# A two-layer decoder trunk on one core: the mixing of the gating layer moved between its products, with its first weights, first tile and norm row handled earlier

## The chip, the core and the metric

The kernel runs on one core of a Trainium2 chip. Time is the device time of one execution, in microseconds (us). The engines that matter are TensorE (PE, matrix products; its weight loads are shown as PEld), VectorE (DVE), ScalarE (ACT), GpSimd (POOL), and SyncE (SP), which here only starts transfers. Each engine runs its own instructions in the order in which they are written and waits at counters (semaphores) that the others raise.

## The reference

A decoder trunk with two layers on 512 positions of width 1024. Layer 0 mixes with attention and gated linear attention, layer 1 with the spatial gating below (`w_in` is 1024 x 4096, u and v have 2048 columns each). Each layer then has cross-attention into a memory of 256 rows and a mixture of 16 experts of which each position uses two. An RMS norm stands before every part.

```python
def sgu_mixer(h, w_in, ln_g, ln_b, ws, bs, w_out):
    B, S = h.shape[:2]
    z = jax.nn.gelu(h @ w_in)
    u, v = z[..., :SG_WIDTH], z[..., SG_WIDTH:]
    v = layernorm(v, ln_g, ln_b).reshape(B, S // SG_CHUNK, SG_CHUNK, SG_GROUPS, SG_GW)
    w_causal = ws * jnp.tril(jnp.ones((SG_CHUNK, SG_CHUNK), ws.dtype))
    mixed = jnp.einsum('gts,bnsgc->bntgc', w_causal, v) + bs.T[None, None, :, :, None]
    return (u * mixed.reshape(B, S, SG_WIDTH)) @ w_out

for layer in range(DEPTH):
    h = rmsnorm(x, norm_mix[layer])
...
        mix = sgu_mixer(h, sg_w_in[i], sg_ln_g[i], sg_ln_b[i], sg_ws[i], sg_bs[i], sg_w_out[i])
    x = x + mix
...
```

## The kernel before

Positions lie in T = 4 tiles of 128. Every large product is taken in three terms: weights and activations are split into a rounded part (hi) and the rest (lo), and `product` (L222 to L239) issues hi·hi, hi·lo and lo·hi. Weights come in groups of 1024 x 512, in two halves h = 0, 1. SP loads a half into `w_stage` once the lo of the group before it is out (`load`), ACT copies it to `w_hi` once PE has used the half before (`split_hi`, L175; one half alone in `half_hi`, L193), and DVE subtracts it into `w_lo` (`split_lo`, L185; `half_lo`, L199). A product reads 4 tiles x 2 halves, 12 matmuls each. In the text, P0 to P7 are the eight products with `sg_w_in` (P0 to P3 give v, P4 to P7 give u, transposed), and P8 to P11 the four with `sg_w_out`.

The experts of layer 0 (`moe_experts`) end in a loop over extra blocks. After it ACT and DVE each write half of the last result (`finish`), POOL scatters it, and when all is stored SP and ACT load the eight blocks of result rows back (`Combine.load`, L1679).

The gating layer (`sgu_layer`) is one block of code, in which it then does this. ACT and DVE split the weights of P0. DVE adds the result rows to `x_res` (L1692, two adds a tile), ACT squares a tile (L1714) and takes the root (L1720), DVE divides (L1726) and scales by the norm's row (L1728), PE turns the tile (L1740), ACT copies it out (hi, L2184) and DVE subtracts (lo, L2224). On ACT the square and root of tile i + 1 stand ahead of the copy of tile i. P0 works through tiles and halves in a mixed order. Behind each product ACT applies the gelu (L2210, L2213). After P3 the mean and variance of v are taken (ACT squares, L2202), DVE centres v (L2251), POOL multiplies by the layer norm's gain (L2151) and DVE adds its bias (L2256, L2260), with the splits of the coming weights between these. After P7, PE transposes the masked mixing weights `sgu_ws` (L2176) and ACT copies them (L2216).

A second block follows: PE makes the 16 mixing units (L2272, four 128 x 128 matmuls each), DVE adds the mixing bias (L2280) and multiplies by u (L2284), ACT rounds (um_hi, L2290) and POOL subtracts (um_lo, L2296). All engines meet at the end of each block before any starts the next. Then `into_queries` runs P8 to P11, adds them to `x_res`, and goes on to the queries of the cross-attention. `NormTiles` is also used there, and at the start of each mixture of experts (`moe_front`).

## Time and profile before

| | us |
|---|---|
| median of 3 runs (1768.4 to 1770.33) | 1770.12 |
| the profiled execution, its own time | 1771.84 |
| its span, first to last instruction | 1769.8 |
| TensorE busy in the span | 1503.7 (85%) |
| VectorE busy | 991.4 (56%) |
| ScalarE busy | 771.4 (44%) |
| mean granted TensorE clock | 0.914 of full |

The span is the stretch that the trace covers; the execution is 2.0 us longer. The busy shares are averages over very different stages: the gating layer, from the experts' last product at 961 us to the end of P11 at 1309 us, is only a fifth of the span. Times in rows are microseconds from the start of the span.

### The profile page before, as it was taken

To read this page: it belongs to the slowest core of one execution; us is meant where nothing else is said; L and a number is where in the kernel's file an instruction comes from. 1 tells how busy PE (TensorE), PEld (TensorE's weight loads), DVE (VectorE), ACT (ScalarE), POOL (GpSimd) and SP (SyncE) were. 2 spreads that over 40 slices of the span, in tenths; PEclk is the share of its full clock that TensorE was granted. 3 is DMA by queue.
4 is the path that set the end of the run, shared out by engine and by line. 5 is a ranking of instruction groups with operands and counts; after the bars stand their busy time and mean duration, and the time that the engine had idled before them with its cause. 6 is when DMAs were issued, how large, how long until landed. Compare 5 with 4: busy or idle time off the path is not lost. (4 is left out here: it accounts for less than half of the span.)

```text
span 1769.8 us, 19447 instructions
## 1 busy us (share of the span) xinstructions
PE 1503.7 (85%) x7649; PEld 1242.2 (70%) x7649; DVE 991.4 (56%) x1299; ACT 771.4 (44%) x1133; POOL 156.5 (9%) x173
## 2 busy tenths in 40 slices
PE   5789689889899895699996799797989894899994
PEld 4577566667678564699995588676877473899983
DVE  3156447574634526588993522734234526699974
ACT  3222345474423513477773322422133513677761
POOL 1000011200000000111211000504000000121111
PEclk8899799878999997799998799898999897899997
DMA  6523021022342052599994342213212043699985
GB/s 185 83 74 98 2 98 49 1 96 96 113 164 72 1 209 107 179 351 373 366 358 166 118 174 95 71 48 123 90 64 72 0 168 125 227 367 370 369 329 197
DMA packets 105981, 276.52 MB, mean 156 GB/s; under 512 B 36625, under 2 KB 39074, under 8 KB 101026
## 3 DMA queue, kind: packets, MB, share of 16 engines
q1 hardware_dynamic: 69922, 203.68, 32.3%
q10 hardware_dynamic: 26464, 54.79, 8.9%
q0 software_dynamic: 9504, 16.80, 2.5%
q8 instruction: 61, 1.00, 0.2%
q14 instruction: 30, 0.25, 0.0%
HBM read 267.83 MB, written 25.17 MB: 166 GB/s over the span
## 5 line engine op out<-in xcount | busy, mean ns | idle before, releaser
L185 DVE TENSOR_TENSOR w_lo<-w_stage,w_hi 128x2048 fp32r<-128x2048 f32 (+2 forms) x48 | 112.0, 2345 | 307.8 <-ACT w_hi L175 291.6
L175 ACT ACTIVATE w_hi<-w_stage 128x2048 fp32r<-128x2048 f32 (+2 forms) x48 | 86.4, 1812 | 334.7 <-PE bank L239 207.3
L2617 ACT ACTIVATE w_lo<-e_room 128x1536 fp32r<-128x1536 f32 x60 | 89.3, 1488 | 87.1 <-DMA e_room<-in_moe_w_in 85.0
L2621 DVE TENSOR_TENSOR e_wi_lo<-e_room,w_hi 128x1536 fp32r<-128x1536 f32 x60 | 102.9, 1749 | 27.1 <-ACT w_hi L2617 27.1
L2621 DVE TENSOR_TENSOR e_wi_lo<-e_room,w_lo 128x1536 fp32r<-128x1536 f32 x60 | 105.3, 1755 | 20.1 <-ACT w_lo L2617 19.7
L2617 ACT ACTIVATE w_hi<-e_room 128x1536 fp32r<-128x1536 f32 x60 | 86.9, 1500 | 31.9 <-PE bank L239 18.4
L2732 PE MATMUL bank<-e_wi_lo,e_hx_hi 128*128 128x384 f32 x256 | 87.2, 341 | 0.0
L193 ACT ACTIVATE w_hi<-w_stage 128x2048 fp32r<-128x2048 f32 x26 | 49.6, 1913 | 85.6 <-PE bank L239 63.5
L2731 PE MATMUL bank<-e_wi_lo,e_hx_hi 128*128 128x384 f32 x256 | 86.6, 338 | 0.0
L199 DVE TENSOR_TENSOR w_lo<-w_stage,w_hi 128x2048 fp32r<-128x2048 f32 x26 | 59.5, 2288 | 44.1 <-ACT w_hi L193 37.7
L239 PE MATMUL bank<-w_hi,h_mix_hi 128*128 128x512 f32 x128 | 53.3, 416 | 21.4 <-DVE w_lo L185 12.0
L2722 PE MATMUL bank<-ident,e_tok 128*128 128x128 f32 x272 | 40.5, 295 | 25.3 <-PEq L2354 19.8
L236 PE MATMUL bank<-h_sg_hi,w_hi 128*128 128x512 f32 x128 | 51.9, 405 | 10.1 <-DVE w_lo L185 10.1
L239 PE MATMUL bank<-w_hi,um_hi 128*128 128x512 f32 x128 | 51.8, 404 | 9.7 <-PEq L2265 9.7
L2812 ACT ACTIVATE e_hx_hi<-bank 128x512 fp32r<-128x512 f32 x68 | 36.8, 596 | 51.1 <-PE bank L2722 51.0
L2722 PEld LDWEIGHTS bank<-ident,e_tok 128*128 128x128 f32 x272 | 39.1, 207 | 27.9 <-issue 25.8
L2901 DVE TENSOR_TENSOR e_hx_lo<-bank,e_hx_hi 128x512 fp32r<-128x512 f32 x68 | 43.5, 682 | 26.2 <-ACT e_hx_hi L2812 26.2
L2680 POOL DMA_INDIRECT moe_y<-e_tok,moe_slots x28 | 28.1, 1002 | 335.8 <-DVE e_tok L2918 309.7
L2625 POOL DMA_INDIRECT e_tok<-moe_h,moe_slots x32 | 39.5, 1235 | 198.3 <-DVE moe_slots L2574 143.7
L997 PEld LDWEIGHTS bank<-v_sw,probT 128*128 128x128 f32 x304 | 38.1, 194 | 23.3 <-ACT probT L1027 11.6
L239 PE MATMUL bank<-w_hi,x_o_hi 128*128 128x512 f32 x128 | 50.7, 396 | 3.4 <-PEq L1998 3.4
L2731 PE MATMUL bank<-w_hi,e_hx_hi 128*128 128x384 f32 x128 | 48.4, 378 | 5.0 <-DVE e_hx_lo L2901 5.0
(512 smaller groups left out, 4226.4 us busy)
## 6 DMA issues: line engine op xcount, KB each, us to landing
e_room<-in_moe_w_in SPq DMA_DIRECT2D x128, 768.0 KB, 7.7
e_wo<-in_moe_w_out ACTq DMA_DIRECT2D x16, 1536.0 KB, 10.2
e_room<-in_moe_w_out ACTq DMA_DIRECT2D x14, 1536.0 KB, 11.1
w_stage<-in_x_wkv SPq DMA_DIRECT2D x16, 1024.0 KB, 5.1
w_stage<-in_sg_w_in SPq DMA_DIRECT2D x16, 1024.0 KB, 5.4
w_stage<-in_hyb_w_in SPq DMA_DIRECT2D x10, 1024.0 KB, 5.3
w_stage<-in_x_wq SPq DMA_DIRECT2D x8, 1024.0 KB, 5.0
w_stage<-in_x_wo SPq DMA_DIRECT2D x8, 1024.0 KB, 6.0
```

Source lines behind the costliest of these rows:

```text
L175: act.activation(self.w_hi[h][:, :, :cols], self.stage[h][:, :, :cols], ACT.Copy)\
L185: dve.tensor_tensor(self.w_lo[h][:, :, :cols], self.stage[h][:, :, :cols], self.w_hi[h][:, :, :cols], ALU.subtract).then_inc(self.lo_done[ ...
L193: act.activation(self.w_hi[h][:, :, :cols], self.stage[h][:, :, :cols], ACT.Copy).then_inc(self.hi_done[h], 1)
L199: engine.tensor_tensor(self.w_lo[h][:, :, :cols], self.stage[h][:, :, :cols], self.w_hi[h][:, :, :cols], ALU.subtract).then_inc(self.lo_do ...
L236: ins = pe.matmul(banks[b][:w_cols.stop - w_cols.start, :tiles * P], w_part[:, kk, w_cols], x_part[:, k, :tiles * P], start=start, stop=stop)
L239: ins = pe.matmul(banks[b][:, :cols], x_part[:, k, b * P:(b + 1) * P], w_part[:, kk, :cols], start=start, stop=stop)
L2617: act.activation(self.hi[q], self.raw[q][:, :, :], ACT.Copy).then_inc(self.wi_his[q], 1)
L2621: dve.tensor_tensor(self.lo[q][:, :, :], self.raw[q][:, :, :], self.hi[q], ALU.subtract).then_inc(self.wi_los[q], 1)
L2722: ins = pe.transpose(turn_ps[k // 4][:, (k % 4) * P:(k % 4 + 1) * P], hx[:, j, k // KC * KC * P + k % KC:(k // KC + 1) * KC * P:KC], m.ide ...
L2731: pe.matmul(gate_ps[:, 0:DE], x[:, k, :], wt[q][:, kk, 0:DE], start=start, stop=stop)
L2732: ins = pe.matmul(up_ps[:, 0:DE], x[:, k, :], wt[q][:, kk, DE:2 * DE], start=start, stop=stop)
L2901: ins = dve.tensor_tensor(hx_lo[j][:, 4 * g:4 * g + 4, :], turn_ps[g][:, :].rearrange("p (k t) -> p k t", k=4), hx_hi[j][:, 4 * g:4 * g + ...
```

## The change

All of it is in and around the gating layer of layer 1.

1. The 16 mixing units go between the tiles of P5, P6 and P7: units 0 to 3, 4 to 7 and 8 to 15. Their results use the PSUM banks of the product before, units 12 to 15 the banks of units 8 to 11 again. DVE applies bias and gate per unit, ACT and DVE then split, in the same block. The last product's gelu stays in PSUM. POOL has no part in it any more.
2. The layer norm's gain and bias are no longer applied to v. They are loaded as columns (16 numbers in each of 128 partitions), and applied after the mixing, where a column is one channel: mixed · gain + (row sums of the mixing weights · bias + mixing bias). The row sums are two products with ones, in P2, where the transposes of `sgu_ws` now stand too.
3. P8 is begun in the same block, and P9's weights are split in it.
4. P0's weights are split by ACT and DVE at the experts' end, ahead of their `finish`.
5. In P0 each tile is normed, turned, split and multiplied before the next: ACT copies tile i before it squares tile i + 1, DVE takes its lo before the next norm, and PE takes both halves of a tile in a row.
6. The norm's row is loaded before the result rows, into the experts' room. The other small loads wait for the rows, and stand ahead of P1's weights.
7. A first square root on a spare number (`ready_root`) is issued ahead of the norm, here, in `into_queries` and in `moe_front`.
8. P5's weights are taken by DVE behind the statistics, one half between the centrings.

```diff
@@ NormTiles, Residual, Combine
+    def load_gain(self, engine, gain):
+        engine.dma_start(self.gain_row, gain.partition_broadcast(P)).then_inc(self.m.next_gain_in, 16)
+
+    def landed(self, engine):
+        for j in self.ORDER[-2:]:
+            engine.wait_ge(self.m.y_in[j], 16 * (self.layer + 1))
...
+    def ready_root(self, act):
+
+        act.wait_ge(self.eps_set, 1)
+        act.activation(self.spare[:, 0:1], self.eps[:, 0:1], ACT.Sqrt)
...
@@ sgu_layer, sync
-                    nt.load(sp, a["norm_mix"][layer])
+                    combine.landed(sp)
                     sp.dma_start(ws[:, :, :], a["sg_ws"][0].rearrange("g t s -> t g s")).then_inc(ws_in, 16)
+                    with nc.allow_non_contiguous_dma(reason="one gain and one bias per partition"):
+                        sp.dma_start(gcol[:, :], a["sg_ln_g"][0].rearrange("(k p) -> p k", p=P)).then_inc(small_in, 16)
+                        sp.dma_start(bcol[:, :], a["sg_ln_b"][0].rearrange("(k p) -> p k", p=P)).then_inc(small_in, 16)
+                    sp.dma_start(bsr[:, :, :], a["sg_bs"][0].partition_broadcast(P)).then_inc(small_in, 16)
                     m.load(sp, first + NGR)
...
@@ gpsimd
-                    pool.wait_ge(small_in, 48)
-                    for i in range(T):
-                        pool.wait_ge(centred, i + 1)
-                        pool.tensor_tensor(v[:, i, :], v[:, i, :], g[:, :], ALU.mult).then_inc(gained, 1)
+                    pool.memset(ones[:, :], 1.0).then_inc(ws_masked, 1)
@@ tensor
                     turn(0)
-                    turn(1)
                     m.product(pe, first, False, bank(0), hi, lo, ahead=ahead,
-                              order=[(0, 0), (1, 0), (0, 1), (1, 1), (0, 2), (0, 3), (1, 2), (1, 3)])
+                              order=[(h, b) for b in range(T) for h in range(2)])
+                    def mix(k):
+
+                        if k < 12:
+                            pe.wait_ge(read, 4 * NGR + k + 1)
+                        if k == 0:
+                            pe.wait_ge(centred, T)
+                        if k >= 12:
+                            pe.wait_ge(gated, min(k - 3, 12))
+                        for i in range(T):
+                            ins = pe.matmul(bank(NGR + min(k, 11) // 4)[k % 4][:, i * P:(i + 1) * P], v[:, i, k * P:(k + 1) * P],
+                                            wsT[:, k * SGG // KU, :], start=True, stop=True)
+                        ins.then_inc(mixed, 1)
...
+                    between = {2: turn_mix, NGR + 1: mixes({1: [0], 2: [1], 3: [2], 4: [3]}),
+                               NGR + 2: mixes({1: [4], 2: [5], 3: [6], 4: [7]}),
+                               NGR + 3: mixes({1: [8], 2: [9], 3: [10], 4: [11, 12], 5: [13], 6: [14], 7: [15]})}
...
+                    def begin(h, b):
+                        if h == 0:
+                            pe.wait_ge(um_los, KD)
+                            pe.wait_ge(gated, 12 + b + 1)
+
+                    m.product(pe, first + 2 * NGR, False, m.psum[0:4], um_hi, um_lo, last=False, ahead=begin)
@@ scalar
-                    m.split_hi(act, first)
-                    nt.square(act, 0)
-                    nt.take_root(act, 0)
-                    for i in range(1, T):
+                    nt.ready_root(act)
+                    for i in range(T):
                         nt.square(act, i)
                         nt.take_root(act, i)
-                        keep_norm(i - 1)
-                    keep_norm(T - 1)
+                        keep_norm(i)
...
+                        elif n == LAST:
+                            m.half_hi(act, first + n + 1, 1)
+                            part_hi(8, KU)
+                    m.split_hi(act, first + 2 * NGR + 1)
@@ vector
+                    def add_bias(k):
+
+
+                        dve.wait_ge(mixed, k + 1)
...
+                        dve.scalar_tensor_tensor(out=bias[:, k % 2, :], in0=ws[:, gr, :], scalar=bcol[:, k:k + 1], in1=bsr[:, gr, :],
+                                                 op0=ALU.mult, op1=ALU.add).then_inc(bias_made, 1)
...
+                        dve.scalar_tensor_tensor(out=out.rearrange("p (i t) -> p i t", i=T), in0=ps.rearrange("p (i t) -> p i t", i=T),
+                                                 scalar=gcol[:, k:k + 1], in1=bias[:, k % 2, :].unsqueeze(1).to_broadcast([P, T, P]),
+                                                 op0=ALU.mult, op1=ALU.add).then_inc(biased, 1)
...
+                    m.split_lo(dve, first + 2 * NGR + 1)
-        with nc.Block() as block:
-            @block.tensor
-            def _(pe):
-                for k in range(KU):
...
@@ moe_experts, scalar (and the same with split_lo in vector)
                 n = rest(act)
+                if upcoming is not None:
+                    m.split_hi(act, upcoming)
                 act.wait_ge(wo_used, n + L)
```

What stands on three engines where the orders differ. On ACT, from the experts' last result to the first tile of the gating layer (`e_tok` holds the experts' result, `w_stage` the loaded weights, `h_sg_hi` the turned tile), before:

```order
L2834 ACTIVATE e_tok<-bank 128x512
L1679 DMA e_room<-moe_y 128x1024 x4
L2662 UNCONDITIONAL_BRANCH
L2179 UNCONDITIONAL_BRANCH
L175 ACTIVATE w_hi<-w_stage 128x2048 x2
L1714 ACTIVATE sg_v,sg_n_ms<-x_res 128x1024
L1720 ACT_TABLE_LOAD
L1720 ACTIVATE sg_n_root<-sg_n_ms,sg_n_eps 128x1
L1714 ACTIVATE sg_v,sg_n_ms<-x_res 128x1024
L1720 ACTIVATE sg_n_root<-sg_n_ms,sg_n_eps 128x1
L2184 ACTIVATE h_sg_hi<-bank 128x4x128 x2
```

and now:

```order
L175 ACTIVATE w_hi<-w_stage 128x2048 x2
L2996 REGISTER_ALU
L2937 ACTIVATE e_tok<-bank 128x512
L1682 DMA e_room<-moe_y 128x1024 x4
L2761 UNCONDITIONAL_BRANCH
L2245 UNCONDITIONAL_BRANCH
L1726 ACT_TABLE_LOAD
L1726 ACTIVATE sg_n_spare<-sg_n_eps 128x1
L1730 ACTIVATE sg_v,sg_n_ms<-x_res 128x1024
L1734 ACTIVATE sg_n_root<-sg_n_ms,sg_n_eps 128x1
L2250 ACTIVATE h_sg_hi<-bank 128x4x128 x2
```

The two copies of the weights stand ahead of the last result, a table load and a square root ahead of the first square, and the copy of tile 0 ahead of the square of tile 1.

On DVE, from the statistics after P3 (`sg_nmean`, `sg_var`) on, before:

```order
L2243 TENSOR_REDUCE sg_nmean<-sg_vsum 128x4
L2244 TENSOR_SCALAR sg_nmean<-sg_nmean 128x4
L185 TENSOR_TENSOR w_lo<-w_stage,w_hi 128x2048 x2
L2247 TENSOR_SCALAR sg_var<-sg_var 128x4
L2249 RECIPROCAL sg_var<-sg_root 128x4
L2251 TENSOR_SCALAR sg_v<-sg_v,sg_nmean,sg_var 128x2048 x4
L185 TENSOR_TENSOR w_lo<-w_stage,w_hi 128x2048 x2
L2256 TENSOR_TENSOR sg_v<-sg_v,sgu_b 128x2048 x2
L185 TENSOR_TENSOR w_lo<-w_stage,w_hi 128x2048 x2
L2260 TENSOR_TENSOR sg_v<-sg_v,sgu_b 128x2048 x2
L185 TENSOR_TENSOR w_lo<-w_stage,w_hi 128x2048 x2
```

and now (`sg_bias` is the bias of one unit, `bank` its mixing result, `uT` the gelu of u):

```order
L2330 TENSOR_REDUCE sg_nmean<-sg_vsum 128x4
L2331 TENSOR_SCALAR sg_nmean<-sg_nmean 128x4
L2333 TENSOR_SCALAR sg_var<-sg_var 128x4
L2335 RECIPROCAL sg_var<-sg_root 128x4
L2338 TENSOR_SCALAR sg_v<-sg_v,sg_nmean,sg_var 128x2048
L199 TENSOR_TENSOR w_lo<-w_stage,w_hi 128x2048
L2338 TENSOR_SCALAR sg_v<-sg_v,sg_nmean,sg_var 128x2048 x3
L199 TENSOR_TENSOR w_lo<-w_stage,w_hi 128x2048
L2350 SCALAR_TENSOR_TENSOR sg_bias<-sgu_ws,sgu_b,sg_bs_row 128x128
L2355 SCALAR_TENSOR_TENSOR bank<-bank,sgu_g,sg_bias 128x512
L2363 TENSOR_TENSOR uT<-uT,bank 128x512
L2350 SCALAR_TENSOR_TENSOR sg_bias<-sgu_ws,sgu_b,sg_bs_row 128x128
```

P5's weights moved behind the statistics, the bias adds over 2048 columns are gone, and the first units come before P6's weights.

On PE, where the gating block ended before (`sg_wsT` holds the transposed mixing weights):

```order
L236 MATMUL bank<-h_sg_lo,w_hi 128x512
L2176 MATMUL bank<-ident,sgu_ws 128x128 x8
L2129 UNCONDITIONAL_BRANCH
L2266 UNCONDITIONAL_BRANCH
L2272 MATMUL bank<-sg_wsT,sg_v 128x128 x64
L2265 UNCONDITIONAL_BRANCH
L1789 UNCONDITIONAL_BRANCH
L239 MATMUL bank<-w_hi,um_hi 128x512
L239 MATMUL bank<-w_lo,um_hi 128x512
L239 MATMUL bank<-w_hi,um_lo 128x512
```

and where it ends now, at the last row of P8 and the first of P9:

```order
L239 MATMUL bank<-w_hi,um_lo 128x512
L2155 UNCONDITIONAL_BRANCH
L1803 UNCONDITIONAL_BRANCH
L239 MATMUL bank<-w_hi,h_sg_hi 128x512
L239 MATMUL bank<-w_lo,h_sg_hi 128x512
L239 MATMUL bank<-w_hi,h_sg_lo 128x512
```

The transposes and the 64 mixing matmuls no longer stand between two ends of blocks; one end of a block is left, between P8 and P9, instead of two ahead of P8.

## Rows read from the trace of the kernel before

**Rows 1.** ScalarE, timeline: start, us, instruction, times, idle before it.

```profile
955.17 0.50 ACT L2819 ACTIVATE e_actT<-bank 128x384 f32<-128x384 f32 x1
...
969.27 3.71 ACT L175 ACTIVATE w_hi<-w_stage 128x2048 fp32r<-128x2048 f32 x2 [7.24 <-PEq L2662]
...
979.57 1.28 ACT L1720 ACT_TABLE_LOAD   x1
980.87 0.29 ACT L1720 ACTIVATE sg_n_root<-sg_n_ms,sg_n_eps 128x1 f32<-128x1 f32 x1
...
986.40 1.06 ACT L2184 ACTIVATE h_sg_hi<-bank 128x512 fp32r<-128x512 f32 x2
```

**Rows 2.** VectorE, timeline.

```profile
961.44 0.69 DVE L2918 COPY e_tok<-bank 128x512 f32<-128x512 f32 x1 [4.83 <-PE bank L2743]
971.22 4.49 DVE L185 TENSOR_TENSOR w_lo<-w_stage,w_hi 128x2048 fp32r<-128x2048 f32 x2 [9.09 <-ACT w_hi L175]
975.62 3.88 DVE L1692 SCALAR_TENSOR_TENSOR x_res<-e_room,moe_wgt,x_res 128x1024 f32<-128x1024 f32 x3
...
989.12 1.28 DVE L2224 TENSOR_TENSOR h_sg_lo<-bank,h_sg_hi 128x512 fp32r<-128x512 f32 x2
...
1131.92 13.13 DVE L185 TENSOR_TENSOR w_lo<-w_stage,w_hi 128x2048 fp32r<-128x2048 f32 x2
```

**Rows 3.** The first result rows' transfers, issued at 966.2 us: time to landing.

```profile
DMA to landing us min/median/max: 4.5/4.6/4.8
```

**Rows 4.** The last result rows' transfers, issued at 967.5 us: time to landing.

```profile
DMA to landing us min/median/max: 8.9/10.1/11.3
```

**Rows 5.** Table loads of the norms' roots: ns min/median/max, first and last start.

```profile
L1720 ACT ACT_TABLE_LOAD  x4: 1283/1283/1283, 673.6 to 1464.1; - x4
```

**Rows 6.** TensorE, timeline, at its waits and one product's start.

```profile
983.00 1.97 PE L1740 MATMUL bank<-ident,sg_v 128*128 128x128 f32 x8 [21.61 <-DVE sg_v L1728]
...
990.55 0.77 PE L239 MATMUL bank<-w_hi,h_sg_hi 128*128 128x512 f32 x1 [0.51 <-DVE h_sg_lo L2224]
...
1138.64 0.77 PE L236 MATMUL bank<-h_sg_hi,w_hi 128*128 128x512 f32 x1 [10.07 <-DVE w_lo L185]
...
1191.50 16.16 PE L2272 MATMUL bank<-sg_wsT,sg_v 128*128 128x128 f32 x128 [4.35 <-PEq L2129]
...
1217.34 0.77 PE L239 MATMUL bank<-w_hi,um_hi 128*128 128x512 f32 x1 [9.68 <-PEq L2265]
```

**Rows 7.** Windows: us, busy of PE, PEld, DVE, ACT, POOL, clock, DMA share, GB/s.

```profile
1016.60:1106.20 89.60, 89.60 (x385) 72.09 (x384) 18.68 (x10) 25.96 (x41) 0.00 (x0) 1.00 0.40 135
...
1138.60:1144.00 5.40, 5.36 (x13) 4.23 (x14) 5.40 (x1) 0.00 (x0) 4.30 (x1) 0.50 0.58 194
...
1217.30:1222.40 5.10, 5.06 (x12) 4.03 (x13) 0.00 (x0) 0.00 (x0) 0.10 (x1) 0.50 0.79 182
```

**Rows 8.** Windows of the mixing units alone (L2272): PE, PEld, clock, DMA.

```profile
1193.50:1194.50 1.00, 1.00 (x7) 1.00 (x7) 0.50 0.00 0
...
1202.00:1204.00 2.00, 2.00 (x20) 2.00 (x19) 1.00 0.00 0
```

**Rows 9.** The centring's instructions: ns min/median/max.

```profile
L2251 DVE TENSOR_SCALAR sg_v<-sg_v,sg_nmean,sg_var x4: 1341/3468/5656, 1118.3 to 1126.4; 128x2048 f32<-128x2048 f32 x4
```

**Rows 10.** Groups by line, 960 to 1320 us: busy us, mean ns; idle before.

```profile
L2280 DVE TENSOR_TENSOR bank<-bank,sg_bs_row 128x512 f32<-128x512 f32 x16 | 11.1, 693 | 2.7 <-PE bank L2272 2.7
...
L2213 ACT ACTIVATE uT<-bank 128x512 f32<-128x512 f32 x16 | 8.2, 597 | 0.0
```

**Rows 11.** DMA issues of the whole run: count, KB each, us to landing.

```profile
w_stage<-in_sg_w_in SPq DMA_DIRECT2D x16, 1024.0 KB, 5.4
...
mem_gains<-in_norm_mem ACTq DMA_DIRECT2D x2, 4.0 KB, 6.7
k_gains<-in_x_knorm ACTq DMA_DIRECT2D x2, 1.0 KB, 6.5
...
mix_gain<-in_norm_mix SPq DMA_DIRECT2D x1, 4.0 KB, 10.6
```

More of the change, by code:

```diff
@@ L1757, in into_queries @@
         out = xn
-        res = Residual(m, f"{nm}_mix", first, parts, x_in)
+        res = Residual(m, f"{nm}_mix", first, parts, x_in, begun=back is not None)
         nt = NormTiles(m, f"{nm}_n", t, res, xn, gb)
@@ new lines, in turn_mix @@
+                    def turn_mix(h, b):
+                        if (h, b) == (0, 2):
+                            pe.wait_ge(read, 8)
+                            pe.wait_ge(ws_masked, 2)
+                            for q in range(2):
+                                for j in range(4):
+                                    ins = pe.transpose(bank(1)[q][:, j * P:(j + 1) * P], ws[:, 4 * q + j, :], m.ident[:, :])
+                                ins.then_inc(turned, 1)
+                        if (h, b) == (1, 1):
+                            pe.wait_ge(ws_out, 2)
+                            for q in range(2):
+                                ins = pe.matmul(bank(1)[2 + q][:, :], ones[:, :], wsT[:, 4 * q:4 * q + 4, :].rearrange("p g t -> p (g t)"),
+                                                start=True, stop=True)
+                            ins.then_inc(summed, 1)
@@ new lines, in gate, with part_lo @@
+                    def gate(k):
+                        dve.wait_ge(biased, k + 1)
+                        dve.wait_ge(read, 4 * NGR + k + 1)
+                        other = bank(NGR + k // 4)[k % 4][:, :]
+                        dve.tensor_tensor(uT[:, k, :], uT[:, k, :], other, ALU.mult).then_inc(gated, 1)
+                    def part_lo(k0, k1):
+                        for k in range(k0, k1):
+                            dve.wait_ge(um_his, k + 1)
+                            dve.tensor_tensor(half(k)[1], uT[:, k, :], half(k)[0], ALU.subtract).then_inc(um_los, 1)
@@ L2253, in _ @@
+                    centre(0)
+                    m.half_lo(dve, first + NGR + 1, 0)
+                    for i in range(1, T):
+                        centre(i)
+                    m.half_lo(dve, first + NGR + 1, 1)
+                    for k in range(4):
+                        add_bias(k)
+                        gate(k)
                     m.split_lo(dve, first + NGR + 2)
-                    for i in range(2):
-                        dve.wait_ge(gained, i + 1)
-                        dve.tensor_tensor(v[:, i, :], v[:, i, :], b[:, :], ALU.add)
+                    for k in range(4, 8):
+                        add_bias(k)
+                        gate(k)
@@ L2257, in _ @@
+                    part_lo(0, 4)
                     m.split_lo(dve, first + NGR + 3)
-                    for i in range(2, T):
-                        dve.wait_ge(gained, i + 1)
-                        dve.tensor_tensor(v[:, i, :], v[:, i, :], b[:, :], ALU.add)
-                    m.split_lo(dve, first + 2 * NGR)
-        um_hi, um_lo = m.split_pair(um_ctx, "um", k=KU, side="right")
-        m.phase()
-        mixed, biased, gated, split, lo_out = (m.psem(f"sg_{s}") for s in ("mixed", "biased", "gated", "split", "lo_out"))
@@ new lines, in _ @@
+                    for k in range(8, 12):
+                        add_bias(k)
+                        gate(k)
+                    part_lo(4, 8)
+                    m.half_lo(dve, first + 2 * NGR, 0)
+                    for k in range(12, KU):
+                        add_bias(k)
+                    for k in range(12, KU):
+                        gate(k)
+                    m.half_lo(dve, first + 2 * NGR, 1)
+                    part_lo(8, KU)
+                    m.split_lo(dve, first + 2 * NGR + 1)
```

172 lines of the change are left out of this document (94 added, 78 removed).

## The prediction, made before the change was run

> **What bounds the kernel now.** I read first where TensorE waits in the stretch from the experts' last product (it ends at 961.4 us) to P8, with the timelines of ScalarE and VectorE beside it, then the windows for the clock. Inside P1 to P4 nothing waits: four products take 89.6 us, 22.4 each, at the full 2.4 GHz [rows 7]. What can be won lies at four places, which rows 6 show by their waits: 21.61 us ahead of the first tile, some 6 more to P0 at 990.55; 10.07 us ahead of P6; and 4.35 and 9.68 us on either side of the mixing. After the 10 us waits the clock is at its low level, 1.2 GHz, for 5.4 and 5.1 us [rows 7]; even the 4.35 us wait is followed by low clock within the mixing [rows 8].
>
> The first place is a chain. The result rows are issued at 966.2 and the first two land 4.6 us later, at 970.8 [rows 3], but VectorE adds them at 975.62, straight behind 4.49 us of weight split that itself waited for ScalarE's 3.71 us [rows 1, 2]. Then come a square, a table load of 1.28 us and the root [rows 1, 5]. PE turns tile 0 from 983.00 to 984.97 [rows 6], ScalarE copies it only at 986.40 [rows 1], behind the square of tile 1, VectorE takes the lo only at 989.12 [rows 2], behind tile 1's norm and an add. The third place: four centrings of 3.5 us mean, of which the shortest, begun before GpSimd's multiplies, took 1.34 [rows 9], and then 13.13 us for two splits [rows 2] that take 4.49 elsewhere. So two engines that work at the same time on large float32 tiles slow one another here, and P6 waits for it. The fourth is a serial section of two ends of blocks.
>
> **The change part by part.** Savings are counted as how much earlier a product starts.
>
> Start of P0. After the loop ScalarE is free at 955.67 [rows 1]. Its 3.71 us of copies, VectorE's last half of 2.25 behind them, and up to 1 us to leave the loop end at 961.6 to 962.6. The last result's `finish` waits behind them on both engines, and it could start at 961.44 [rows 2]; POOL's scatter and both row queues wait for it in turn. That is a delay of 0.2 to 1.2 us, and I take 1.3, since the scatter's own start may not align. The first add then comes at 970.8 + 1.3 + 0.3 = 972.4 instead of 975.6: 3.2. The table load, issued while the rows are under way, gives 1.3. From the end of tile 0's transposes to P0 there were 990.55 - 984.97 = 5.6 us; in the new order two copies (1.06 together, rows 1), the second half of a lo (0.68, half of the 1.28 in rows 2) and handovers make about 2.1: 3.5. Sum: 8.0, so P0 starts near 982.6. The norm's row leaves the chain, but the root came later than it did.
>
> P0 itself. Its start at the low clock stays. One more transposition lies inside it (half of 1.97 at full clock, rows 6): -1.0. The rest of a tile's chain (square, root, scale, copy, lo) is about 5 us against 5.6 us of products per tile, so I take no wait, and up to 2 as the bad end. The order by tiles releases half 0 of the weights only 2.8 us before P0's end instead of 5.6, and copy and split take 1.9 + 2.3 + 0.15: P1 waits 1.55 longer. Left: 5.4.
>
> P2: eight transposes moved in (1.0) and two products with ones, each of 512 columns as a whole mixing unit, 0.8: -2.6. Left: 2.8. VectorE's two copies of the sums and the waits on the small loads are hidden by P2's second half, 8 us.
>
> P4 to P7. A mixing unit is eight records, ten records take 1 us at the full clock [rows 8]: 0.8 us, 16 units, 12.8 in all. Unit 0 also waits for P4's first gelu: the copy of P5's second half 1.9, a table load 1.3 and a gelu 0.6 [rows 10] after P4's end, against 2.8 us of products, so 1.2. After P5: 2.8 - 3.2 - 1.2 = -1.6. The centrings at 1.34 are over before P4 ends, and one half split between them is ready for P5. P6's weights then come behind unit 3, with 7 us to spare: the 10.07 us wait goes, and with it half of 5.4 at the low clock, 2.7. Left: 11.2 at P6's start, and after the twelve units in P6 and P7 (9.6) 1.6. So P7 ends near 1184.5, against 1186.1.
>
> VectorE's load there: per unit a small bias, then two passes of 0.69 [rows 10], 1.7 us; PE gives one per 3.6. It is hidden while P5 to P7 run. GpSimd's 16 subtractions move to VectorE, where 8 fit into P6 and P7 and 8 into P8.
>
> The serial section. From 1186.1 to P8's start at 1217.34 are 31.2 us, and half of 5.1 at the low clock is 2.6 [rows 6, 7]. Now P8 waits only for the gelu (0.6) and the gate (0.7) of unit 12, with handovers 1.5. Left: 1.6 + 31.2 + 2.6 - 1.5 = 33.9.
>
> **A wait that the change adds.** P9's second half of weights can be copied only when P8 has used its own, so copy 1.9, split 2.3 and the end of the block (0.5) and SP's last issue (0.4) follow P8's end with PE idle, though half 0 is ready: -5.1. All queues wait there. After 4.35 us there were about 3 us of low clock [rows 8], after 10.07 there were 5.4 [rows 7]; between the two I take 3.4, half of it lost: -1.7. Left: 27.1.
>
> The other roots. Two `moe_front` and the `into_queries` of layer 1 have a table load in the chain of tile 0 (four in rows 5, one of them the gating layer's own), with PE idle soon behind. 3 x 1.28 = 3.8, less 0.2 where the last tile's add waits for PE: 3.6.
>
> Small loads. P1's weights were needed at 1011 and now at 1006.6, when P0's half 0 is free. SP starts them behind the last rows, 967.5 + 11.3 + 1.3 = 980.1 [rows 4], behind four small loads. A column load has 2048 separate numbers. Loads of 1024 and of 256 separate numbers landed after 6.7 and 6.5 us [rows 11], so nearly all of it is latency that overlaps. At 6.7 each and strictly one after another, weights would land at 980.1 + 4 x 6.7 + 5.4 = 1012.3, 5.7 late. Overlapped they are in time; I take 0, and 5.7 as the end of the range.
>
> **Sum**: 27.1 + 3.6 = 30.7. The profiled execution took 1771.84, so 1741.1; the median lies 1.7 lower, so 1739.4.
>
> **Rivals.** *The columns are late.* One after another, as above, or one of them at the 10.6 us of a load queued behind 4 MB [rows 11]: +5.7, 1745.1. Against it, SP's transfers overlapped in every stage. *The columns cost by the number* (this one ends slower). If the 6.5 us of the 256 numbers were their price, 2048 cost 52 us, and two 104; P1's weights land at 1090, 83 us after they are needed, and the kernel takes 1739.4 + 83 = 1822. It decides from about 26 us a load. Against it stands the load of 1024 numbers in 6.7. The Trainium skill, "DMA: Bandwidth & Descriptors", Rules for kernel authors, speaks against such a load: a last dimension that isn't contiguous becomes one descriptor per element, and one is told to rearrange. By that rule there are 2048 descriptors a load here; the rows show no price for one beyond latency. *The norms' 3.6 us are taken back* by a transfer that the experts wait for: 1743. *The units wait.* PE takes its work in order, and each unit stands behind a gelu of the product before or a gate; at 0.5 us for each of 16 the kernel takes 8 more, 1747.4. Against it, VectorE needs 1.7 us of 3.6. *A table switch costs more than its record.* If each switch cost its record twice, four of them would give 5.1 more: 1734.3. Against it, the root starts at 980.87, 0.02 us behind the table's end [rows 1]. The Trainium skill ("ScalarE: Activation LUTs", What ACT_TABLE_LOAD costs) gives about 2.66 us for every switch, 1.28 and a drain; by that the four are worth 10.6 rather than 5.1.
>
> **How the numbers follow.** Forecast 0.58 (own range 1736 to 1743), norms taken back 0.14, columns late 0.10, units wait 0.08, table 0.04, columns by the number or a like jam 0.03, and 0.03 for a change whose parts give each other nothing. A measurement of this kernel can tell some 0.2%, 3.5 us, from no change. Faster by more: 0.95; within: 0.02; slower: 0.03. The range takes the table's 1734.3 at the low end, and 1745 with part of the norms or of the units' waits at the high end: 1733.5 to 1748. It leaves out the last two cases and the worst sums.
>
> **What would show it.** P0 should start 8 us earlier relative to the experts' last product, P1 show one wait of 1.5 us, P5 to P7 last 26.8, 25.6 and 28.8 us at full clock with no wait for weights, P8 start 1.5 us after P7, and one wait of 5 us stand between P8 and P9 with low clock behind it. VectorE's centrings should take 1.3 us each. No table load should stand between a square and a root. A wait of PE for weights ahead of P1 longer than 3 us would show the columns late; waits spread over P5 to P7 would show the units; P8 at a low clock would mean that I priced the handover too low. If P6 still waits for its weights, then it was not GpSimd that slowed VectorE.

## The result, and the profile of the changed kernel

| | before | changed |
|---|---|---|
| median of 4 runs, us | 1769.26 (1766.39 to 1770.33) | 1739.65 (1735.79 to 1745.9) |
| the profiled execution, its own time | 1771.84 | 1736.91 |
| its span | 1769.8 | 1735.1 |
| TensorE busy in the span | 1503.7 (85%) | 1493.7 (86%) |
| VectorE busy | 991.4 | 983.2 |
| mean granted TensorE clock | 0.914 | 0.927 |

The ratio is 0.9844, with a 95% interval of 0.9821 to 0.9866: 27.6 us less than 1769.26 by the ratio, 23.7 to 31.7 by its interval, and 29.6 between the medians. Forecast were 1739.4 and 30.7 us.

The timeline of TensorE in the changed kernel, at its waits. Columns: start in us, duration in us, instruction, result from inputs, times, and in brackets the idle time ahead of it with what ended it. These rows answer to [rows 6].

```profile
951.37 5.39 PE L2846 MATMUL bank<-e_wo,e_actT 128*128 128x512 f32 x12 [1.01 <-ACT e_actT L2922]
973.05 1.97 PE L1754 MATMUL bank<-ident,sg_v 128*128 128x128 f32 x8 [16.29 <-DVE sg_v L1742]
977.12 0.77 PE L239 MATMUL bank<-w_hi,h_sg_hi 128*128 128x512 f32 x1 [2.10 <-DVE h_sg_lo L2306]
1005.85 0.50 PE L239 MATMUL bank<-w_hi,h_sg_hi 128*128 128x512 f32 x1 [1.60 <-DVE w_lo L185]
1102.26 1.16 PE L2200 MATMUL bank<-sg_wsT,sg_v 128*128 128x128 f32 x8 [1.17 <-ACT uT L2290]
1182.65 0.47 PE L239 MATMUL bank<-w_hi,um_hi 128*128 128x512 f32 x1 [1.55 <-DVE uT L2363]
1210.50 0.77 PE L239 MATMUL bank<-w_hi,h_sg_hi 128*128 128x512 f32 x1 [5.22 <-PEq L2155]
1284.66 1.60 PE L1754 MATMUL bank<-ident,x_xn 128*128 128x128 f32 x8 [3.68 <-DVE x_h_lo L1908]
```

Read from the top: the experts' last product, tile 0's turn, P0, P1, mixing unit 0 (inside P5), P8, P9, and a tile's turn behind P11. The waits of 21.61, 10.07, 4.35 and 9.68 us of [rows 6] have become 16.29, nothing, nothing and 1.55, and there is one new wait of 5.22.

The products between them are told by windows of the changed kernel: P5, P6 and P7. Columns: stretch, its length, busy time of PE, PEld, DVE, ACT and POOL with instructions, granted clock, DMA share, GB/s.

```profile
1098.40:1125.80 27.40, 26.23 (x130) 21.55 (x129) 11.84 (x15) 7.19 (x8) 0.00 (x0) 1.00 0.28 90
1125.80:1151.70 25.90, 25.90 (x130) 21.50 (x129) 14.00 (x18) 7.82 (x10) 0.00 (x0) 1.00 0.26 82
1151.70:1181.10 29.40, 29.40 (x160) 24.74 (x158) 18.14 (x26) 7.85 (x10) 0.00 (x0) 1.00 0.21 73
```

The clock is at 2.4 GHz throughout (1.00), and P6 and P7 have no idle time. VectorE is busy for 12 to 18 us of each. Its centrings answer to [rows 9] (min/median/max in ns), and the first one and one half of P5's split stand where the order puts them:

```profile
L2338 DVE TENSOR_SCALAR sg_v<-sg_v,sg_nmean,sg_var x4: 1341/1342/1347, 1090.9 to 1097.2; 128x2048 f32<-128x2048 f32 x4
1090.90 1.35 DVE L2338 TENSOR_SCALAR sg_v<-sg_v,sg_nmean,sg_var 128x2048 f32<-128x2048 f32 x1
1092.49 2.29 DVE L199 TENSOR_TENSOR w_lo<-w_stage,w_hi 128x2048 fp32r<-128x2048 f32 x1 [0.24 <-ACT w_hi L175]
```

**One clock for all kernels.** Between two executions the times from the start of the span drift, so I count from the start of the experts' last product (956.01 and 951.37 here, the rows with L2743 and L2846). The earlier 4.64 us are then set apart. "Turn" is the last row of the first fence.

| us behind the experts' last product | P0 | P8 | P9 | turn |
|---|---|---|---|---|
| before | 34.5 | 261.3 | 286.5 | 360.5 |
| changed | 25.8 | 231.3 | 259.1 | 333.3 |
| less | 8.8 | 30.1 | 27.4 | 27.2 |

Of the 27.2 us, 1.3 are the table load of the norm behind P11, so the gating layer gave 25.9. The norms outside it gave 1.3 each: TensorE's rows of the two kernels are 36.8 us apart ahead of layer 1's `moe_front` and 38.2 behind its norm, and 0.8 and 2.1 in layer 0. That is 25.9 + 3.9 = 29.8 us, and the medians differ by 29.6; the ratio gives 27.6, so the agreement to 0.2 us is partly chance. The two profiled executions are 34.9 apart, and the rest is not the change's. 2.5 us arose inside layer 0's experts, whose code is the same: TensorE's stretch from their first turn to their last product took 238.1 us in the profiled execution of before, 235.6 in that of the changed kernel, and 235.4 to 238.3 in the twelve kernels below. Another 5.0 us arose in layer 1's cross-attention, between the turn (31.8 us apart) and the 36.8, where the same 16 transposes took 3.39 us before and 1.97 now, and 3.4 us went back behind the last norm.

### The profile page after: what moved, and what is told of

The parts are those of the page before. It is cut to its first block and busy times, and to the rows that moved or that the text cites. A ratio compares the mean times of both kernels' runs of the same rounds, so it can differ in the third digit from the quotient of the medians.

```text
span 1735.1 us, 19494 instructions
## 1 busy us (share of the span) xinstructions
PE 1493.7 (86%) x7653; PEld 1233.3 (71%) x7653; DVE 983.2 (57%) x1329; ACT 770.5 (44%) x1138; POOL 114.0 (7%) x154
## 2 busy tenths in 40 slices
DMA packets 109822, 274.44 MB, mean 158 GB/s; under 512 B 40722, under 2 KB 43171, under 8 KB 105123
## 5 line engine op out<-in xcount | busy, mean ns | idle before, releaser
L185 DVE TENSOR_TENSOR w_lo<-w_stage,w_hi 128x2048 fp32r<-128x2048 f32 (+2 forms) x42 | 89.7, 2148 | 244.2 <-ACT w_hi L175 227.1
L175 ACT ACTIVATE w_hi<-w_stage 128x2048 fp32r<-128x2048 f32 (+2 forms) x46 | 82.5, 1807 | 297.6 <-PE bank L239 201.2
L199 DVE TENSOR_TENSOR w_lo<-w_stage,w_hi 128x2048 fp32r<-128x2048 f32 x32 | 73.3, 2289 | 64.4 <-ACT w_hi L193 37.2
L193 ACT ACTIVATE w_hi<-w_stage 128x2048 fp32r<-128x2048 f32 x28 | 53.5, 1913 | 93.1 <-PE bank L239 62.2
L239 PE MATMUL bank<-w_hi,h_sg_hi 128*128 128x512 f32 x192 | 78.3, 408 | 8.9 <-PEq L2155 5.2
L239 PE MATMUL bank<-w_lo,h_sg_hi 128*128 128x512 f32 x192 | 77.0, 401 | 0.0
L239 PE MATMUL bank<-w_hi,h_sg_lo 128*128 128x512 f32 x192 | 77.0, 401 | 0.0
L2825 PEld LDWEIGHTS bank<-ident,e_tok 128*128 128x128 f32 x272 | 38.7, 207 | 27.9 <-issue 25.8
```

Source lines behind the costliest of these rows:

```text
L175: act.activation(self.w_hi[h][:, :, :cols], self.stage[h][:, :, :cols], ACT.Copy)\
L185: dve.tensor_tensor(self.w_lo[h][:, :, :cols], self.stage[h][:, :, :cols], self.w_hi[h][:, :, :cols], ALU.subtract).then_inc(self.lo_done[ ...
L193: act.activation(self.w_hi[h][:, :, :cols], self.stage[h][:, :, :cols], ACT.Copy).then_inc(self.hi_done[h], 1)
L199: engine.tensor_tensor(self.w_lo[h][:, :, :cols], self.stage[h][:, :, :cols], self.w_hi[h][:, :, :cols], ALU.subtract).then_inc(self.lo_do ...
L239: ins = pe.matmul(banks[b][:, :cols], x_part[:, k, b * P:(b + 1) * P], w_part[:, kk, :cols], start=start, stop=stop)
L2825: ins = pe.transpose(turn_ps[k // 4][:, (k % 4) * P:(k % 4 + 1) * P], hx[:, j, k // KC * KC * P + k % KC:(k // KC + 1) * KC * P:KC], m.ide ...
```

## The experiments

**The changed kernel once more**

> The changed kernel once more, as the other end for the kernels that are run beside it. The sum of the prediction gives a ratio of 0.983 to the kernel before (30.7 us less); if part of the 34.9 us between the two profiled executions was chance (3.3 us stand ahead of the gating layer in the trace, of which the table load ahead of the first mixture of experts explains 1.3), the ratio stays at 0.983 and does not go to 0.980.

1739.91 us, ratio 0.9841 (0.9816 to 0.9866). P0, P8, P9 and the turn stand at 25.9, 231.4, 259.2 and 333.4 us on the common clock: here the stage repeats to 0.1 us, although the times of whole executions spread over 12 us. It does not always. In two kernels further down the same order of work stands ahead of P8, and P8 starts at 232.0 and 232.4 us, because the low clock at P0's start lasted 5.6 and 6.2 us instead of 4.1. The turn moves by another 1.5 us with the low clock in P9. So effects of two microseconds and more are read below from that clock, those under 1.2 us are not shown by one pair of traces, and the ratio is used only where effects are large.

**The mixing in a row, in the same block**

```diff
-                    between = {2: turn_mix, NGR + 1: mixes({1: [0], ...
+                    between = {2: turn_mix}
...
+                    for k in range(KU):
+                        mix(k)
```

The units use the banks of P6 in turn; VectorE takes all splits first, then biases and gates, then the differences.

> The changed kernel, but all 16 mixing units stand in a row behind P7, still in the same block and still with the columns and VectorE's differences: only the interleaving is undone. Theory: P5 to P7 fall from 27.4, 25.9 and 29.4 us to 22.4 us each (15.5 us back), and behind P7 VectorE does 16 units of 0.35 + 0.75 + 0.65 us and 8 differences of 0.6 us before P8 can begin, 33 us in place of a wait of 1.6 us, with a low clock behind it (1 to 3 us): 17 to 20 us more than the changed kernel, ratio to the kernel before about 0.994. Rival: the 27 us that the gating layer lost came from the dropped block ends and GpSimd's part, not from the interleaving: less than 8 us more than the changed kernel, ratio under 0.989.

1766.71 us, ratio 0.9998 (0.9985 to 1.0011): nearly the whole gain is gone, 24.4 us of it by the common clock at P9 and 25.6 at the turn (P0, P8, P9, turn: 25.7, 253.5, 283.6, 358.9). The rival is dead: it gave the interleaving less than 8 us. All other parts of the change are in this kernel, and they leave it at the time of before. P0 still starts 8.8 us earlier than before and P6 waits for nothing, but P8 starts only 7.8 us earlier, and behind P9's wait, which stays, 1.6 are left at the turn. My size, 17 to 20 us, was short by some 6. VectorE's timeline behind P7, which ended at 1162.7:

```profile
1166.61 2.29 DVE L199 TENSOR_TENSOR w_lo<-w_stage,w_hi 128x2048 fp32r<-128x2048 f32 x1 [10.79 <-ACT w_hi L193]
1168.82 0.35 DVE L2343 SCALAR_TENSOR_TENSOR sg_bias<-sgu_ws,sgu_b,sg_bs_row 128x128 f32<-128x128 f32 x1
1197.26 4.89 DVE L2361 TENSOR_TENSOR um_lo<-uT,um_hi 128x512 fp32r<-128x512 f32 x8
```

The first unit's bias comes 6.1 us behind P7, because half 1 of P8's weights, which ScalarE copies only after the gelu, stood ahead of it in VectorE's order. Then come 28.4 us for 16 units, 1.78 each, and 4.9 of differences. P8 started at 1202.25, 39.6 us behind P7 and not 33. I had written the queue and not walked it.

**GpSimd's multiplication left out of the kernel before**

```diff
-                        pool.wait_ge(centred, i + 1)
-                        pool.tensor_tensor(v[:, i, :], v[:, i, :], g[:, :], ALU.mult).then_inc(gained, 1)
```

> The kernel before without the multiplication of v by the layer norm's gain, which GpSimd did beside VectorE's centrings: this work is left out and nothing takes its place. Theory: the centrings took 1.34 to 5.66 us each because GpSimd worked beside them; without it each takes 1.34 us, VectorE reaches the split of P6's weights some 8 us earlier, and the 10.07 us wait at P6 falls to 0 to 2 us: 8 to 10 us less. Rival: the wait at P6 comes from the order of VectorE's work (statistics, split of P5, centrings, bias in a row); then it stays over 5 us.

1755.54 us, ratio 0.9931 (0.9908 to 0.9954), some 12 us less, where I had expected 8 to 10 and left out the low clock behind the wait. VectorE, and below it, from the kernel before, the same instructions and GpSimd's:

```profile
1116.07 5.12 DVE L2247 TENSOR_SCALAR sg_v<-sg_v,sg_nmean,sg_var 128x2048 f32<-128x2048 f32 x4
1121.10 2.29 DVE L185 TENSOR_TENSOR w_lo<-w_stage,w_hi 128x2048 fp32r<-128x2048 f32 x1
```

```profile
1118.31 13.68 DVE L2251 TENSOR_SCALAR sg_v<-sg_v,sg_nmean,sg_var 128x2048 f32<-128x2048 f32 x4
1131.92 13.13 DVE L185 TENSOR_TENSOR w_lo<-w_stage,w_hi 128x2048 fp32r<-128x2048 f32 x2
1119.82 23.08 POOL L2151 TENSOR_TENSOR sg_v<-sg_v,sgu_g 128x2048 f32<-128x2048 f32 x4 [135.91 <-DVE sg_v L2251]
```

Four centrings take 5.12 us in place of 13.68, and TensorE waits for nothing from P1 to the mixing. From the second tile's turn to the mixing it took 190.8 us (985.55 to 1176.34) in place of 203.4: 12.6, which is the 10.07 of the wait and the 2.7 of the low clock behind it. The order of VectorE's work was the same, so the rival is dead. The Trainium skill, "SBUF — State Buffer", SBUF: two separate sides, has GpSimd share one pair of ports with VectorE as an exclusive lock: where VectorE runs in a two-port mode, or reads two inputs from SBUF beside a GpSimd operation that reads SBUF, one engine stands still for a whole instruction of the other. The trace agrees in kind: the longest centring took 4.3 us more than the shortest, and all of it went with GpSimd's work; the lock itself no run here shows.

**The spare root alone, in the kernel before**

```diff
+                nt.ready_root(act)
                 for i in range(3):
                     nt.square(act, i)
```

> The kernel before with the spare square root alone, ahead of all norms (gating layer, queries twice, mixtures of experts twice). Theory: each table load of 1.28 us that stands between the first square and its root goes into idle time of ScalarE, and each is on the path: five times 1.3, or 6.4 us less, the queries of layer 0 counted only if they wait for the root; the prediction took 4.9 us (1.3 in the gating layer, 3.6 for three of the others), ratio 0.9972. Rival: a load costs more than its own 1.28 us because the engine drains around it, 2.7 us each: 10 to 13 us less, ratio 0.994. Other rival: the loads only move (the next gelu or exponential must load its table anyway), ratio 1.000.

1762.7 us, ratio 0.9972 (0.9958 to 0.9986), 4.9 us less: the predicted sum of 1.3 and 3.6. The price of a drain (10 us and more) lies outside the interval, and so does a mere move of the loads. In the gating layer only 0.8 us arrived at the first turn (978.94 - 952.72 = 26.2 against 27.0) and 1.2 at P0. VectorE's row says why:

```profile
977.40 0.16 DVE L1728 RECIPROCAL sg_n_rstd<-sg_n_root 128x1 f32<-128x1 f32 x1 [1.18 <-DMA sg_junk<-in_norm_mix]
```

With the table load gone the norm's row is the last to come. The Trainium skill, "ScalarE: Activation LUTs", What ACT_TABLE_LOAD costs, gives 2.66 us a switch, 1.28 of them the load; what a hidden load brought here was 1.3 us at each of three norms, the load alone.

**The norm's row asked for in the gating block again**

```diff
-                    combine.load_gain(sp, m.a["norm_mix"][layer + 1])
...
+                    combine.load_gain(sp, a["norm_mix"][layer])
                     combine.landed(sp)
```

> The changed kernel, but the norm's row is asked for at the start of the gating block again, behind SyncE's four result rows. Theory: in the kernel before with the spare root alone, the first norm then waited 1.2 us for this row, although VectorE's adds ended late there (976.2); in the changed kernel the adds end 11 us earlier against the request, so the row (7 to 8 us from its request, some 1.7 us behind the rows' own) is the last to come: the first norm waits 1.5 to 3 us and P0 starts that much later than 25.8 us behind the experts' last product; the time is 1.5 to 3 us over the changed kernel. Rival: the row lands beside the result rows and costs nothing.

P0 at 31.0 us in place of 25.8, P8 at 236.3 in place of 231.3: 5.2 and 5.0 us more, over the 3 that I gave it at most. The timing (0.9855, 0.983 to 0.988) does not contradict that and does not show it. The row took 11.2 us from its request at 966.33, behind eight result rows of the same size, not 7 to 8:

```profile
977.53 0.16 DVE L1740 RECIPROCAL sg_n_rstd<-sg_n_root 128x1 f32<-128x1 f32 x1 [5.81 <-DMA e_room<-in_norm_mix]
```

**P0's weights split in the gating block again**

```diff
-                    m.split_hi(act, upcoming)
...
+                    m.split_hi(act, first)
                     nt.ready_root(act)
...
+                    m.split_lo(dve, first)
                     combine.add(dve, 0, 0)
```

> The changed kernel with P0's weights split in the gating block again, ahead of the norm. Theory: VectorE adds the first row only after 4.5 us of splits, P0 starts 3.4 us later than the 25.8 us behind the experts' last product, less the 1.0 us by which the rows are asked for sooner since the result's last half isn't queued behind the split: 3.2 us more. Rival: the rows' landing, 4 us behind their request, hides most of the split: under 1 us more.

P0 at 29.8 us, P8 at 235.2: 4.0 and 3.9 us more than the changed kernel; 1744.17 us, ratio 0.9865 (0.9844 to 0.9887). The theory holds with a term that was 0.8 us too small; the rival does not.

**P0's old order**

```diff
-                              order=[(h, b) for b in range(T) for h in range(2)])
+                              order=[(0, 0), (1, 0), (0, 1), (1, 1), (0, 2), (0, 3), (1, 2), (1, 3)])
```

with the turns, copies and norms in the order of before.

> The changed kernel with P0's order as it was before (two tiles turned ahead, root of the next tile ahead of the copy, mixed halves). Theory: P0 starts 3.5 us later against the experts' last product (29.2 us behind its start in place of 25.8), but P0 has no turn more inside it and P1 no wait of 1.6 us, which gives 2.6 us back: the time is that of the changed kernel within 1.5 us (the net of the term was 1.0 us). Rival: the order is worth its full 3.5 us.

P0 at 28.5 us, 2.75 later; but P8 at 230.8, 0.5 us earlier. Ratio 0.9844 (0.9822 to 0.9865), that of the changed kernel. Part 5 of the change gives nothing that can be seen: the earlier start is paid back inside P0 and at P1. Which of the two orders is ahead is not shown, because the low clock at P0's start was not equally long. Windows from 3 to 6 us behind P0's start, of this kernel and of the changed one:

```profile
983.19:986.19 3.00, 3.00 (x14) 2.36 (x14) 2.63 (x5) 1.45 (x3) 0.00 (x0) 0.98 0.99 338
980.12:983.12 3.00, 3.00 (x16) 2.48 (x16) 2.13 (x2) 0.18 (x1) 1.20 (x2) 0.81 1.02 180
```

A granted clock of 0.81 in place of 0.98 over 3 us is the whole 0.5 us.

**Eight more columns**

```diff
+                        for j in range(8):
+                            sp.dma_start(more[:, j, :], a["sg_ln_g"][0].rearrange("(k p) -> p k", p=P)).then_inc(more_in, 16)
```

> The changed kernel with eight more loads of the gain's column behind the two that it has, ahead of P1's weights in SyncE's queue; nothing reads them. The second column held SyncE for 2.7 us. Theory: a column load costs its queue 2.5 to 3 us, eight push the request for P1's weights from 5.0 us behind the first small load to some 26 us, past the 16 us of slack that P1's weights have, and P1 waits 4 to 8 us for them. Rival: the column loads run beside the rest at well under 1 us each (the first took 0.58 us): P1 waits 1.6 us as before. Other rival: a column costs by its 2048 numbers, over 8 us each: P1 waits over 40 us.

SyncE's own timeline:

```profile
974.79 2.76 SPq L2163 DMA_DIRECT2D sgu_b<-in_sg_ln_b  x1
977.59 11.35 SPq L2165 DMA_DIRECT2D sg_wsT<-in_sg_ln_g  x8
989.00 1.36 SPq L2166 DMA_DIRECT2D sg_bs_row<-in_sg_bs  x1
990.41 67.17 SPq L163 DMA_DIRECT2D w_stage<-in_sg_w_in  x8
```

Eight loads held the queue for 11.35 us, 1.4 each, where I had expected 2.5 to 3: the 2.7 us of the second column were not the price of a column. By the common clock P1's weights were asked for 11.7 us later than in the changed kernel, the first half landed some 5.5 us on, near 996, and P1 still waited 1.60 us, for the split. The one execution of this kernel took 1733.48 us. The theory fails, and so does the price by the number; the first rival had the wait right and its price, well under 1 us, too low. A column is cheap enough that ten are hidden. The Trainium skill, "DMA: Bandwidth & Descriptors", Rules for kernel authors, warns of one descriptor for each number. The trace agrees on the count: this kernel moved 57233 packets under 512 B and the changed one 40722, which is 2064 for each of the eight loads of 2048 numbers. The price in this place was 1.4 us of the queue a load, off the path.

**The wait between P8 and P9 closed.** Only half 0 of P9's weights is split in the gating block; half 1 moves to the next block, whose SyncE loads P10's weights first.

```diff
-                    m.split_lo(dve, first + 2 * NGR + 1)
+                    m.half_lo(dve, first + 2 * NGR + 1, 0)
...
+                if back is not None:
+                    m.half_lo(dve, first + 1, 1)
                 res.split_lo(dve)
```

> The changed kernel, but only one half of P9's weights is split in the block of the gating layer, and the other half in the next block, beside the first half of P9. Theory: the 5.2 us wait between P8 and P9 is the second half of P9's weights, copied only when P8 has used the half before it (0.0 to 4.2 us behind P8's end) and then the meeting of the engines. With half 0 alone the block ends with P8, the wait falls to the 1 to 2 us that a block's end costs elsewhere, and the 3.4 us of low clock behind it (1.7 us lost) goes as well: 3.5 to 5.5 us less than the changed kernel, about 1735. Rival: the wait is the meeting of the engines itself and stays near 5 us, time within 1 us of the changed kernel.

The first row is P9's start; then a window over P9. From the changed kernel stand below them the copy and the split of half 1 behind P8 (which ended near 1205.3), and windows over the first half of its P9 and over its first 2.8 us:

```profile
1202.91 0.47 PE L239 MATMUL bank<-w_hi,h_sg_hi 128*128 128x512 f32 x1 [0.32 <-PEq L2161]
1203.00:1225.60 22.60, 22.60 (x97) 18.17 (x98) 4.58 (x2) 3.78 (x2) 0.10 (x1) 1.00 0.75 262
```

```profile
1205.38 1.91 ACT L175 ACTIVATE w_hi<-w_stage 128x2048 fp32r<-128x2048 f32 x1 [9.28 <-PE bank L239]
1207.32 2.29 DVE L185 TENSOR_TENSOR w_lo<-w_stage,w_hi 128x2048 fp32r<-128x2048 f32 x1 [8.89 <-ACT w_hi L175]
1210.50:1221.20 10.70, 10.70 (x40) 8.57 (x41) 0.00 (x0) 0.00 (x0) 0.10 (x1) 0.87 0.91 351
1210.50:1213.30 2.80, 2.80 (x7) 2.22 (x8) 0.00 (x0) 0.00 (x0) 0.10 (x1) 0.50 0.77 268
```

The wait is 0.32 us in place of 5.22, and the clock over P9 is 1.00, where the changed kernel had 0.87 over 10.7 us, which is 1.4 us lost. At the turn 6.2 us are won (327.1 against 333.3), where I had expected 3.5 to 5.5. 1730.67 us, ratio 0.9784 (0.9759 to 0.9809), against 0.9841 (0.9816 to 0.9866) for the changed kernel beside it: the intervals do not meet, and what the ratios differ by beyond the 6.2 us no row explains. So the meeting of all engines costs 0.3 us where nobody is late, and the 5.2 were half 1.

**The last result ahead of half 1 of P0's split**

```diff
-                    m.split_lo(dve, upcoming)
+                    m.half_lo(dve, upcoming, 0)
                 dve.wait_ge(wo_used, n + L)
...
                 finish(1)
+                if upcoming is not None:
+                    m.half_lo(dve, upcoming, 1)
```

> The changed kernel, but at the experts' end VectorE takes only half 0 of P0's weights ahead of its part of the last result, and half 1 behind it. Theory: VectorE's part of the result starts at the product's end (5.4 us behind its start in place of 6.5), the rows are asked for 10.2 us behind that start in place of 11.2, the split of half 1 lies in the wait for the rows, and P0 starts 24.7 us behind it in place of 25.8: 1.0 us less. Rival: the second half of the split then delays the first add, and P0 starts as late as before or later.

P0 at 26.0 us, not 24.7; ratio 0.9858 (0.9821 to 0.9896). Neither theory had the reason. VectorE did its part of the result 5.4 us behind the product's start instead of 6.5, but then GpSimd's scatter ran beside the split. GpSimd here, and below it in the changed kernel:

```profile
957.91 2.20 POOL L2783 DMA_INDIRECT moe_y<-e_tok,e_ix  x1 [7.57 <-DVE e_tok L3023]
```

```profile
959.35 0.97 POOL L2783 DMA_INDIRECT moe_y<-e_tok,e_ix  x1 [8.52 <-DVE e_tok L3023]
```

It took 2.20 us in place of 0.97, and the split of half 1 (956.98 to 959.26) covers the first 1.35 of them. The rows were asked for 11.4 us behind the product's start, against 11.2. In the two kernels below, which have the same edit, the scatter took 2.20 us as well.

**Two and three edits together**

> The changed kernel with two edits: the wait between P8 and P9 closed as before (6.2 us from P8's start to the last norm's turn), and VectorE's part of the last result ahead of half 1 of P0's split (1.0 us). Theory: they add up, 7 us under the changed kernel, ratio 0.980 to the kernel before, some 1732.

> The same two edits and P0's order as it was before the change. With the changed kernel's other parts this order started P0 2.8 us later and ended P7 0.5 us earlier against the experts' last product; the theory is that this stays so: 0.5 us under the kernel with two edits, which the timing can't tell and the trace can. Rival: with the result rows 1.0 us earlier the tile-first order gains that 1.0 us alone, and this kernel is later by 0.5 us.

1733.34 us, ratio 0.9807 (0.9785 to 0.983), and 1733.21 us, 0.9783 (0.9757 to 0.981). The first expected 7 us under the changed kernel and got 5.1 at the turn (328.2 against 333.3): only the closed wait pays, for the reason just shown. From P8 to the turn both took what the closed kernel took, 95.8 us. From the experts' last product to P8 the tile-first order took 232.4 us and the old order 232.0. That is no proof for the old order: the closed kernel, with the tile-first order, took 231.3. The timing can't tell the three fastest kernels apart. All have the closed wait and are faster than the kernel before; that they are faster than the changed kernel the timing shows for the closed kernel and for the last one, while the interval of the kernel with two edits meets that of the changed kernel, and only the trace speaks for it.

## Why the prediction was right, step by step

The forecast case came: 1739.65 against 1739.4, inside its own range of 1736 to 1743. It was right by its mechanisms, and also because errors of size cancelled. Along the path:

| | forecast | measured |
|---|---|---|
| start of P0 | 8.0 | 8.8 |
| turn in P0 and wait at P1 | -2.55 | -2.7 |
| P2 | -2.6 | -2.6 |
| P5, P6, P7 in us | 26.8, 25.6, 28.8 | 27.4, 25.9, 29.4 |
| P8 behind P7 | 1.5 | 1.55 |
| wait after P8, clock behind it | -5.1, -1.7 | -5.2, about -1.5 |
| gating layer | 27.1 | 25.9 |
| norms outside it | 3.6 | 3.9 |
| sum | 30.7 | 29.8 |

With the measured terms the gating layer comes to 26.3 us instead of 25.9; 0.3 of the difference lies in P1, which took 22.7 us instead of 22.4.

*The start of P0* came term by term. Behind the product's start the first add comes 15.6 us on instead of 19.6, the turn 6.1 behind it instead of 7.4, and P0 4.1 behind the turn instead of 7.6: 4.0, 1.3 and 3.5, where the prediction had 3.2, 1.3 and 3.5. The first add:

```profile
967.00 4.01 DVE L1702 SCALAR_TENSOR_TENSOR x_res<-e_room,moe_wgt,x_res 128x1024 f32<-128x1024 f32 x3 [8.50 <-DMA e_room<-moe_y]
```

Undone one at a time in the changed kernel, the split costs 4.0 and the order 2.75 us at P0, and the table load was worth 1.2 in the kernel before; the norm's row, which the sum gave nothing, costs 5.2. With the row that makes 13.2, where all together gave 8.8: such prices do not add. The step that failed is the sentence that the norm's row "leaves the chain, but the root came later than it did": true of the kernel before, where it therefore got no price. In the changed kernel everything ahead of it had been shortened, and without its earlier request it would have been last, by 5.8 us. My 8.0 held only because part 6 was there, and the working did not say so.

*The delay of the rows* was taken at 1.3 and is 1.0: VectorE's part of the result starts 6.45 us behind the product's start, against 5.43 before.

*The order by tiles* got +3.5 at its start and -2.55 behind it, a net gain of 1.0. The terms measured 2.75 and -3.2, and 0.5 of the second is the length of the low clock at P0's start, which differs from one execution to the next. So the net is near nothing, and the miss is about 1 us.

*The units* were priced at 0.8 us each by the mixing's own records, and took 0.96 in P5 and 0.88 in P6 and P7 (3.8 and 3.5 for four, 7.0 for eight). Over 16 units and with the 1.17 us ahead of unit 0 that is 15.5 us in place of 14.0, the largest miss on the path. The rival, in which the units wait 0.5 us each, would have had 1.3 per unit. The rows place the 0.1: eight records of a unit still take 0.81 us, but the product's first record behind them is followed by the next only after 0.31 us, where 0.23 is the rule. Why, a change of operands or a short handover, was not tried.

```profile
1106.07 1.05 PE L2200 MATMUL bank<-sg_wsT,sg_v 128*128 128x128 f32 x8
1106.88 0.47 PE L236 MATMUL bank<-h_sg_hi,w_hi 128*128 128x512 f32 x1
1107.19 0.39 PE L236 MATMUL bank<-h_sg_hi,w_lo 128*128 128x512 f32 x1
1107.42 0.40 PE L236 MATMUL bank<-h_sg_lo,w_hi 128*128 128x512 f32 x1
```

*GpSimd against VectorE* was the claim that carried 12.8 us, and it is shown by taking the multiplication alone away: 12.6.

*The serial section* was called 31.2 and 2.6 for clock. That the mixing's place decides it is shown by the kernel with the units in a row: back to the time of before.

*The columns* were taken at nothing, with 5.7 us as the end of the range. Ten in a row are still hidden, so that end was far out, and the rival that prices each number is dead by the same run.

*The new wait* was forecast in its cause and size, and the experiment that removes the cause removes 4.9 us of wait and the low clock with it. The norms' 3.6 us were not taken back.

What stays open: the executions of one kernel spread by 2 to 14 us in these runs, often more than any single edit at the gating layer's head brings. I know two sources, the experts' stretch (235.4 to 238.3 us for the same code) and the places where the low clock falls, but not what sets them.

## What to carry to other kernels

Where several late things end together, price a part also by what it would cost to leave it out of the finished change: the norm's row cost nothing in the kernel before and 5.2 us here, where all ahead of it had become shorter. Work of VectorE and of GpSimd on large tiles belongs in different stretches of time where it can be arranged, since here each slowed the other. At a block's end look at the last thing that each engine does there: the meeting itself cost 0.3 us, and what was put ahead of it for the next block's sake cost 5.

## What the runs showed of the hardware

- GpSimd and VectorE slowed one another in both directions: centrings of 1.34 us took up to 5.66 beside a multiplication of GpSimd, and the start of a scatter by GpSimd, 0.97 us, took 2.20 beside a weight split of VectorE.
- A load of 2048 separate numbers into columns held SyncE's queue for 1.4 us in a row of eight, though the second of the first two showed 2.7 us. So a single row of a queue's time need not be the price of the instruction.
- A 512 KB row asked for behind eight result rows of the same size landed 11.2 us after its request, where the rows took 7.8 and 8.2 at the median.
- An idle 5.2 us of TensorE was followed by 2.8 us at 1.2 GHz (granted clock 0.50), an idle 0.32 us in the same place was not (1.00 over all of P9).
